# Two rotations moved forward, gates closed one piece later in two buffers, and the order of the last rows in a transformer of three blocks

## The reference

```python
# first block, layer l
h = rmsnorm(x, g_mix[l])
q_r, k_r, v_r, g_r, q_s, k_s, v_s, gate_a, gate_b = split(h @ w_in[l])
q_r, k_r = rotary(q_r), rotary(k_r) * 128 ** -0.5           # 4 heads of 128
ret = head_group_norm(retention(q_r, k_r, v_r)) * silu(g_r)
sb = stick_breaking(q_s, k_s, v_s)                          # 8 heads of 128
merged = sigmoid(gate_a) * (ret @ p_ret[l]) + sigmoid(gate_b) * (sb @ p_sb[l])
x = x + merged @ w_out[l]
x = x + square(relu(rmsnorm(x, g_mlp[l]) @ w_up[l])) @ w_down[l]
# second block
q, f, i, g, pool = parts of rms_norm(x) @ w_in_2            # 6 heads of 128
o = gated linear recurrence over q, f, i
o = o * rsqrt(mean(o * o)) * norm_g * silu(g)
x = x + concat(pool_mixer(pool), o) @ w_out_2
x = x + square(relu(rms_norm(x) @ w_up_2)) @ w_down_2
```

## Time and profile before

| | |
|---|---|
| time, median of 3 | 1263.89 us (1262.8 to 1266.11) |
| the profiled execution | 1264.06 us, its span 1262.2 us |
| TensorE busy | 1230.4 us, 97% of the span |
| VectorE busy | 882.0 us, 70% |
| ScalarE busy | 630.2 us, 50% |
| GpSimd busy | 53.3 us, 4% |
| mean granted clock of TensorE | 0.996 of full speed |

### The profile page before, as it was taken

One profiled execution on the slowest core, in us unless ns is written; L12 is line 12 of the kernel. 1 busy time (PEld: TensorE's weight loads), 2 busy tenths in 40 slices (PEclk: granted clock), 3 DMA queues, 4 the chain that ended last, 5 costly groups with the idle time before them and its releaser, 6 DMA issues.

```text
span 1262.2 us, 17060 instructions
## 1 busy us (share of the span) xinstructions
PE 1230.4 (97%) x6810; PEld 1062.0 (84%) x6810; DVE 882.0 (70%) x1040; ACT 630.2 (50%) x823; POOL 53.3 (4%) x70
## 2 busy tenths in 40 slices
PE   6999999999999999999999999999989999999998
PEld 4888888888888888888888888888879997888886
DVE  5576887887666676677777877666677766766665
ACT  4455577544434434555677445344358456443342
POOL 1000110001000000000310001000010000100000
PEclk9999999999999999999999999999999999999999
DMA  7754554555555556655555555555646333655652
GB/s 246 251 167 134 166 167 147 188 187 180 181 185 195 177 173 220 184 157 156 153 159 167 177 190 176 191 192 176 214 135 192 108 112 116 199 189 179 197 181 102
DMA packets 163082, 219.85 MB, mean 174 GB/s; under 512 B 5712, under 2 KB 134224, under 8 KB 163024
## 3 DMA queue, kind: packets, MB, share of 16 engines
q1 hardware_dynamic: 163024, 219.04, 54.1%
HBM read 217.98 MB, written 1.05 MB: 174 GB/s over the span
## 4 chain that ended last, share of the span: by engine, by line
PE 59%; issue 19%; DVE 13%; ACT 5%; DMA 2%; POOL 2%; DVEq 0%; SPq 0%; POOLq 0%; ACTq 0%
PE ps L489 59%; DVE w_lo L1292 5%; DVE gtmp L1561 1%; DMA raw<-in_w_in_dram 1%; DVE gates L1304 1%; DVE gtmp L1556 1%; ACT gates L1015 1%; DMA decay_c<-in_decay_dram 1%; ACT w_hi L877 1%; PE ps L521 1%; POOL retqkv L1259 1%; POOL gr L1246 1%; DVE retT L1484 0%; ACT junk L891 0%; DVE ry L1482 0%
## 5 line engine op out<-in xcount | busy, mean ns | idle before, releaser
L489 PE MATMUL ps<-hT,w_hi 128*128 128x512 f32 (+1 forms) x1952 | 592.7, 369 | 3.2 <-DVE hT L1298 3.1
L1292 DVE TENSOR_TENSOR w_lo<-raw,w_hi 128x1024 fp32r<-128x1024 f32 x402 | 477.6, 1231 | 101.0 <-ACT w_hi L877 100.7
L877 ACT ACTIVATE w_hi<-raw 128x1024 fp32r<-128x1024 f32 x402 | 402.3, 1051 | 197.2 <-DMA raw<-in_w_up_dram 130.6
L489 PE MATMUL ps<-hT,w_lo 128*128 128x256 f32 x1696 | 456.9, 281 | 0.0
L489 PEld LDWEIGHTS ps<-hT,w_hi 128*128 128x128 f32 x1952 | 343.0, 190 | 68.9 <-DVE hT L1298 3.6
L489 PEld LDWEIGHTS ps<-hT,w_lo 128*128 128x128 f32 x1696 | 312.5, 189 | 1.8
L489 PE MATMUL ps<-w_hi,uT 128*128 128x512 f32 x768 | 249.3, 397 | 0.0
L883 ACT ACTIVATE carry<-ps 128x512 f32<-128x512 f32 x114 | 67.7, 594 | 238.8 <-PE ps L489 238.7
L489 PEld LDWEIGHTS ps<-w_hi,uT 128*128 128x128 f32 x768 | 144.6, 188 | 35.8 <-DVE uT L1298 1.1
L489 PE MATMUL ps<-w_lo,uT 128*128 128x512 f32 x384 | 152.3, 396 | 0.0
L489 PE MATMUL ps<-w_hi,hT 128*128 128x512 f32 (+1 forms) x480 | 142.4, 374 | 5.7 <-DVE w_lo L1292 4.6
(11 more groups left out here) (185 smaller groups left out, 940.9 us busy)
## 6 DMA issues: line engine op xcount, KB each, us to landing
raw<-in_w_in_dram SPq DMA_DIRECT2D x77, 1024.0 KB, 5.7
raw<-in_w_up_dram SPq DMA_DIRECT2D x48, 1024.0 KB, 5.4
raw<-in_w_down_dram SPq DMA_DIRECT2D x48, 1024.0 KB, 4.9
raw<-in_w_out_dram SPq DMA_DIRECT2D x12, 1024.0 KB, 5.0
raw<-in_p_sb_dram SPq DMA_DIRECT2D x8, 1024.0 KB, 5.2
raw<-in_p_ret_dram SPq DMA_DIRECT2D x8, 1024.0 KB, 5.0
xs<-in_x_dram SPq DMA_DIRECT2D x2, 512.0 KB, 6.1
gain<-in_g_mix_dram SPq DMA_DIRECT2D x2, 512.0 KB, 6.6
```

The source lines that it names most:

```text
L489: return pe.matmul(o, lhsT, rhs, start=start, stop=stop)
L877: act.activation(w_hi[:, s, half], raw[:, s, half], ACT.Copy).then_inc(hi_ready, 1)
L1292: last = dve.tensor_tensor(w_lo[:, s, half], raw[:, s, half], w_hi[:, s, half].bitcast(F32), ALU.subtract)
```

## The change

Three edits.

1. `rotate` 0 goes from piece 18 to 16, `rotate` 1 from 19 to 18. ScalarE's copies no longer wait for `rest_split` and for the last `rk`, but for the last `rq` (queries) or `rk` (keys).
2. `gtmp` gets a second buffer. Of gate n, VectorE's larger-of and ScalarE's last exp are issued with gate n + 1: on VectorE behind the clamp of n + 1 and ahead of the conversion, on ScalarE behind the conversion and ahead of the exp of n + 1. For the last gate they stand at the first piece of `psb`. GpSimd's product for `rg` keeps its place in GpSimd's order. `psb` and `pret` use buffer 0.
3. At piece 11 of the second block ScalarE copies the pool part first, then works out the scales, then rounds part 0 of the rows, and only then does the silu. VectorE does the pool's low parts, `normed(0)`, `gated(0)`, `normed(1)`, `normed(2)`, `gated_lo(0)`, and then `silu_out` and `gated(1)`.

```diff
-        gtmp = place("gtmp", [P, 2, T], F32)
+        gtmp = place("gtmp", [P, 2, 2, T], F32)
...
-        GATES = {"rg": 0, "ga": 4, "gb": 8}
+        GATES = {"rg": 0, "ga": 4, "gb": 8, "psb": 12}
+        GATE_OUT = [None] * 4 + [(0, i) for i in range(4)] + [(1, i) for i in range(4)]
+        def gate_at(kind, i):
+            return GATES[kind] + i
...
-            if k in (18, 19):
-                todo.append(("rotate", k - 18))
+            if k in (16, 18):
+                todo.append(("rotate", (k - 16) // 2))
...
@@ ScalarE, rotate
-                        act.wait_ge(pair_free, use_of("rk", 1, L).count(3))
-                        act.wait_ge(rest_split, Place(3, (L, SB_H // 2)).count(1))
+                        act.wait_ge(pair_free, use_of(("rq", "rk")[i], 1, L).count(3))
...
@@ ScalarE, gates, behind convert(piece + AHEAD)
+                    if kind in ("rg", "ga", "gb") and gate_at(kind, i) or (kind, i) == ("psb", 0):
+                        done = gate_at(kind, i) - 1
+                        g = GATE_OUT[done]
+                        z = gtmp[:, done % 2, :, :]
+                        act.wait_ge(gate_max, Place(done, (L, 12)).count(1))
+                        o = z if g is None else gates[:, g[0], 2 * g[1]:2 * g[1] + 2, :]
+                        act.activation(o, z, ACT.Exp, scale=-1.0).then_inc(gate_sig, 1)
                     if kind in ("rg", "ga", "gb"):
+                        z = gtmp[:, gate_at(kind, i) % 2, :, :]
                         act.wait_ge(gate_clamped, gate.count(1))
-                        act.activation(gtmp[:, :, :], gtmp[:, :, :], ACT.Exp, scale=-1.0).then_inc(gate_exp, 1)
+                        act.activation(z, z, ACT.Exp, scale=-1.0).then_inc(gate_exp, 1)
                         act.wait_ge(gate_exp, gate.count(1))
-                        act.activation(gtmp[:, :, :], gtmp[:, :, :], ACT.Ln, bias=1.0).then_inc(gate_soft, 1)
-                        act.wait_ge(gate_max, gate.count(1))
-                        o = gtmp[:, :, :] if kind == "rg" else gates[:, kind == "gb", 2 * i:2 * i + 2, :]
-                        act.activation(o, gtmp[:, :, :], ACT.Exp, scale=-1.0).then_inc(gate_sig, 1)
+                        act.activation(z, z, ACT.Ln, bias=1.0).then_inc(gate_soft, 1)
...
@@ ScalarE, second block
+            def scale_rows(r):
+                act.wait_ge(o_mean, r + 1)
+                v = o_scale[:, 2 * r:2 * r + 2, :]
+                act.activation(v, ps[:, 4 + r, :].rearrange("p (h t) -> p h t", h=2), ACT.Ln, scale=T / P,
+                               bias=rms_eps[:, 0:1]).then_inc(o_log, 1)
+                act.wait_ge(o_log, r + 1)
+                act.activation(v, v, ACT.Exp, scale=-0.5).then_inc(o_rstd, 1)
+            def round_rows(r):
+                act.wait_ge(o_gated, r + 1)
+                act.activation(yT[:, 2 + 2 * r:4 + 2 * r, 0:T], ho[:, 2 * r:2 * r + 2, :], ACT.Copy).then_inc(o_hi, 1)
...
                 if k == 11:
-                    for r in range(DIAGS):
...
                     act.wait_ge(pool_full, 1)
                     act.wait_ge(cols_in, 64)
                     for b in range(2):
                         act.activation(yT[:, b, 0:T], ps[:, 7, b * T:(b + 1) * T], ACT.Copy,
                                        scale=hcol[:, PSCALE, b:b + 1]).then_inc(pool_hi, 1)
+                    for r in range(DIAGS):
+                        scale_rows(r)
+                    round_rows(0)
...
@@ VectorE, gates
+                def gate_larger(n):
+                    z = gtmp[:, n % 2, :, :]
+                    dve.wait_ge(gate_soft, Place(n, (L, 12)).count(1))
+                    dve.scalar_tensor_tensor(out=z, in0=gate_in(n), scalar=-1.0, in1=z, op0=ALU.mult,
+                                             op1=ALU.max).then_inc(gate_max, 1)
...
                         if kind == "psb" and i == 0:
-                            dve.wait_ge(gate_sig, Place(11, (L, 12)).count(1))
+                            gate_larger(11)
+                            dve.wait_ge(gate_sig, Place(10, (L, 12)).count(1))
...
+                        if kind == "psb" and i == 3:
+                            dve.wait_ge(gate_sig, Place(11, (L, 12)).count(1))
+                        branch = gtmp[:, 0, :, :]
+                        add_cross(use, branch)
...
+                        n = gate_at(kind, i)
                         dve.wait_ge(pair_free, use.count(3))
-                        if gate.fixed:
-                            dve.wait_ge(gate_sig, gate.count(0))
-                        if kind == "rg" and i or kind == "ga" and i == 0:
-                            dve.wait_ge(gate_done, Place(i if kind == "rg" else RET_H, (L, RET_H)).count(0))
-                        dve.tensor_scalar(gtmp[:, :, :], g, GATE_FLOOR, None, ALU.max).then_inc(gate_clamped, 1)
+                        if n >= 2:
+                            dve.wait_ge(gate_sig, Place(n - 2, (L, 12)).count(1))
+                        if 2 <= n < 6:
+                            dve.wait_ge(gate_done, Place(n - 2, (L, RET_H)).count(1))
+                        dve.tensor_scalar(gtmp[:, n % 2, :, :], gate_in(n), GATE_FLOOR, None, ALU.max).then_inc(gate_clamped, 1)
+                        if n:
+                            gate_larger(n - 1)
                     if k < MIX_PIECES - 2:
                         convert(piece + AHEAD)
-                    if gate is not None:
-                        dve.wait_ge(gate_soft, gate.count(1))
-                        dve.scalar_tensor_tensor(out=gtmp[:, :, :], in0=g, scalar=-1.0, in1=gtmp[:, :, :],
-                                                 op0=ALU.mult, op1=ALU.max).then_inc(gate_max, 1)
...
@@ VectorE, second block, piece 11
-                    for r in range(DIAGS):
-                        normed(r)
-                    gated(0)
-                    silu_out(DIAGS + 1, hg[:, h2, :])
                     dve.wait_ge(pool_hi, 2)
...
+                    normed(0)
+                    gated(0)
+                    normed(1)
+                    normed(2)
                     gated_lo(0)
+                    silu_out(DIAGS + 1, hg[:, h2, :])
                     gated(1)
```

More of the change, by code:

```diff
@@ L1181, in _ @@
                     carry_keys(5)
[L1182 to L1185, removed]
+                if k == 12:
+                    round_rows(1)
+                    round_rows(2)
             mlp(Place(6), Place(5), Place(2), Place(first + MIX2_PIECES), Place(use0 + MIX2_USES), False)
@@ L1245, in _ @@
                         g = gr[:, 2 * i:2 * i + 2, :]
-                        pool.tensor_tensor(g, g, gtmp[:, :, :], ALU.mult).then_inc(gate_done, 1)
+                        pool.tensor_tensor(g, g, gtmp[:, i % 2, :, :], ALU.mult).then_inc(gate_done, 1)
                     for name, i in stages(k):
@@ L1486, in stage, with gate_in @@
                         split_lo(retT[:, 2 * i:2 * i + 2, T:2 * T], retT[:, 2 * i:2 * i + 2, 0:T], y).then_inc(ret_lo, 1)
+                def gate_in(n):
+                    g = GATE_OUT[n]
+                    return gr[:, 2 * n:2 * n + 2, :] if g is None else gates[:, g[0], 2 * g[1]:2 * g[1] + 2, :]
+                def gate_larger(n):
[3 more added lines that the diff above has]
+                                             op1=ALU.max).then_inc(gate_max, 1)
                 for k in range(MIX_PIECES):
@@ L1527, in _ @@
                             dve.wait_ge(merged_lo, Place(i - 1, (L, 4)).count(1))
-                        add_cross(use, gtmp[:, :, :])
+                        if kind == "psb" and i == 3:
+                            dve.wait_ge(gate_sig, Place(11, (L, 12)).count(1))
+                        branch = gtmp[:, 0, :, :]
+                        add_cross(use, branch)
                         rows = slice(2 * i, 2 * i + 2)
@@ L1532, in _ @@
                         if kind == "psb":
-                            dve.tensor_tensor(gates[:, 1, rows, :], gates[:, 1, rows, :], gtmp[:, :, :],
+                            dve.tensor_tensor(gates[:, 1, rows, :], gates[:, 1, rows, :], branch,
                                               ALU.mult).then_inc(branch_b, 1)
                         else:
-                            dve.tensor_tensor(gtmp[:, :, :], gates[:, 0, rows, :], gtmp[:, :, :],
+                            dve.tensor_tensor(branch, gates[:, 0, rows, :], branch,
@@ L1537, in _ @@
                                               ALU.mult).then_inc(branch_a, 1)
                             dve.wait_ge(branch_a, part.count(1))
-                            dve.tensor_tensor(gtmp[:, :, :], gates[:, 1, rows, :], gtmp[:, :, :],
+                            dve.tensor_tensor(branch, gates[:, 1, rows, :], branch,
                                               ALU.add).then_inc(merged, 1)
                             dve.wait_ge(merged, part.count(1))
-                            dve.tensor_copy(hT[:, rows, 0:T], gtmp[:, :, :]).then_inc(merged_hi, 1)
```

(18 more changed lines are left out.)

## The result

| | time, us | against before |
|---|---|---|
| before | 1264.18 median (4 runs) | |
| changed | 1270.74 median (1269.44 to 1271.66, 4 runs) | 1.0046, 95% interval 1.0031 to 1.0061 |
| forecast | 1268.9, range 1260.5 to 1272.0 | slower, 0.57 |

The change makes the kernel slower by some 6 us, as forecast. The profiled execution took 1269.44 us with a span of 1267.6.

What follows compares the result with a forecast made beforehand. TensorE, busy 1230.4 of 1262.2 us, was taken to bound the kernel. Terms -2.4 +9.0 +3.0 -1.7 +1.0 -3.9 = +5.0 took the profiled 1264.06 to 1269.1, or 1268.9 against the median; range 1260.5 to 1272.0.

Steps and rivals of the forecast that it cites:

- Keys, -2.4: First block, `ret_scores`: earlier key rotation removes TensorE's wait for rotated keys in both layers, 1.17 + 1.27 us gained.
- `rest_lo`, +9.0: First block, last pair: query rotation at piece 16 delays VectorE's `rest_lo`, stalling TensorE 4.5 us per layer; bounds +4.4, +9.2.
- two readings left open (3.4 or 4.5): `rest_lo` stall per layer: 3.4 us if the second `sb_logs` step overlaps GpSimd's product, 4.5 if they exclude each other.
- Clock, +3.0: TensorE's low clock after each `rest_lo` stall: 1.55 us charged per layer, with 0 and 2.0 each as ends.
- `psb`, -1.7: First block, third piece of `psb`: TensorE's waits for gate work go, 0.46 and 1.26 us.
- GpSimd, +1.0 (0 to 2.2): End of piece 25: sum feeding `ret_var` of head 0 comes late behind `rg` gate 3's product, +0.5 us per layer.
- End, -3.9: Second block's mixer end: `yT` wait (-2.77) and low clock (-1.55) go, 0.4 us returns at the transposes; bounds -4.3, -2.0.
- Rival (a): Clock holds through the `rest_lo` stalls: -3.0, giving 1265.9 us, or about 1264 with a stall of 3.4; chance 0.16.
- (b): Early rotation delays VectorE only by its floor, stall 2.2 us, no low clock: 1260.3 us, middle 1258; chance 0.15.
- (c): Second block's mixer end: `gated_lo(0)` still comes at 1049, so the -3.9 goes: 1273 us; chance 0.07.

Runs made afterwards that it cites:

- the run without the product: Changed kernel with GpSimd's cosine product for the queries left out, ScalarE's copies and both VectorE steps kept: 1264.93 us, 0.9994 of before.
- the sum first: Changed kernel with GpSimd's sum of `rsq` for head 0 issued ahead of the product of `rg` gate 3: 1268.8 us, 1.0032 of before.
- both repairs: Changed kernel with rotations at pieces 17 and 19 and GpSimd's `rsq` sum for head 0 ahead of the `rg` gate 3 product: 1256.06 us, 0.9939 of before.
- the changed kernel again: Changed kernel measured once more with no further edit: 1271.71 us, 1.0058 of before.

## Why the prediction was right, step by step

- **Keys, -2.4.** Right. Each `ret_scores` gains what was worked out, 1.17 and 1.27 from start to start.
- **`rest_lo`, +9.0.** Right, in place and cause; measured 4.29 and 4.28 from start to start, +8.6. VectorE was late by 4.5, against 4.7, and the slack of 0.2 held. Of the two readings left open (3.4 or 4.5), the full exclusion was the true one. That VectorE's own work is half of it and the lock the other half is shown by the run without the product.
- **Clock, +3.0.** The clock did fall, and the size was short, in layer 1 beyond the upper end of 2.0. With matmul set against matmul, layer 0 goes from 5.5 to 7.2 us behind while the clock is low (up to 146.9), +1.7, and layer 1 from 10.2 to 12.8 (up to 611.1), +2.5: +4.2. The other execution of the same kernel lost 3.1 us in each layer. The loss is about half of the part of the low stretch that lies behind the wait: 1.7 of 3.4, 2.5 of 5.3, 3.1 of some 6.6. The premise was weaker than it looked. That 2.61 us "were enough" was one example, and the same wait for `yT` was followed by no low clock in the runs with the rotations alone and with the gates alone. The size was taken from that one example too, so that it came near is in part luck.
- **`psb`, -1.7.** Right: 0.46 and 1.26. Not foreseen: the earlier rotations alone would have brought it as well.
- **GpSimd, +1.0 (0 to 2.2).** The mechanism was right, and I took half of it where the whole came: 1.15 twice, +2.3, a little over the bound of 2.2. The conversion's second half did get in ahead of the sum, in both layers.
- **End, -3.9.** Right against this execution of before: -2.8 for the wait, -1.6 for the clock, +0.5 at the transposes. VectorE's and ScalarE's steps there came within 0.1 us of the working, measured from TensorE's products. But the clock's part is of the execution: in the two runs that kept the `yT` wait no low clock followed it, and against such an execution the end is worth 2.3 us. The run with the end alone gained 3.0, in between.
- **Not in the sum.** The start of the changed execution was 1.2 us later, and a low stretch of clock that the execution of before had at the start of the second block was absent, -1.3. Both are of the execution, not of the edits.

One reading fell short without touching the sum. The prediction counts ScalarE's waits for the larger-of step as 16 and 20.7 us; the kernel before has eight more, for `rg`:

```profile
ACT gtmp L1015 <- DVE gtmp L1561: 11.0, 8, 1.6
```

All 24 are gone in the changed kernel, and by the run with the gates alone no gain that can be told comes of it.

Terms as measured: -2.4 + 8.6 + 4.2 - 1.7 + 2.3 - 3.9 = +7.1. The last point takes off 0.1, and some 1.6 us go in a dozen steps of 0.05 to 0.2 us, which no term of the prediction has. Many of them stand right behind the places above, and the trace names no releaser for most. That makes 5.4, by which the spans differ. So the forecast of +5.0 came close partly because its clock and GpSimd terms were 2.5 us short while these steps, which it left out, took 1.6 us off again. Rival (a) is excluded by the windows, (b) by the two waits of 4.1 us, (c) by the absent `yT` wait.

## What to carry to other kernels

Before work is moved forward on an engine, find the next instruction behind the new place that the bounding engine waits for, and the slack it has: here 0.2 us against 4.5 us of work and waiting, though the engine was only 70% busy over the span. An early result is worth only the wait it removes (1.2 us), its place in the order can cost several times that, and one step later, behind the tight instruction, the same move is free. In an in-order queue with two consumers, the product that nobody waits for soon belongs behind the sum that somebody does.

## What the hardware showed that was not expected

- A scalar_tensor_tensor on VectorE with two SBUF inputs is shut out by a GpSimd product as a tensor_tensor is: 3.09 us instead of 0.96. The one that waits counts as busy in the page.
- The low clock is not set by the length of one wait. Waits of 2.0 us were followed by it in one layer and not in the other of the same execution. The `yT` wait of 2.6 us was followed by it in the kernel before and not in two other runs that have it, and a wait of 2.7 us for `hq` in the run with rotations at 17 and 19 was followed by none. At the start of the second block TensorE waits for `hT` for 1.57, 0.6 and 1.55 us in all twelve profiles alike; the clock falls about the last of these in six of them (before, rotations alone, gates alone, the sum first, both repairs, the changed kernel again), for 3.4 us, and stays high in the other six. Behind the ten waits of 4.0 and 4.1 us for `rest_lo` and `retqkv` it was low every time, for stretches that differed.
- That `hq` wait itself, at the start of the second block, was 1.25 us in the execution of before, and 0.8 to 3.1 in the others, with nothing edited there. I did not look for its cause; it is part of why single executions differ by a few us.
